# Per-head sums of an RWKV branch split into four 64x64 matmuls, and the second branch's first projection moved behind a fourth block of the first

## The reference

```
gates = jax.nn.sigmoid(p[..., i2:].reshape(B, S, N_BRANCH, D))
branch = jnp.einsum('bsnw,nwd->bsnd', ys, w_branch[l])
merged = jnp.sum(gates * branch, axis=2)
```

```
kk = kk / jnp.maximum(jnp.sqrt(jnp.sum(kk * kk, axis=-1, keepdims=True)), 1e-12)      # "length"
mu_y = jnp.mean(y, axis=-1, keepdims=True)                                            # "centre"
var_y = jnp.mean(jnp.square(y - mu_y), axis=-1, keepdims=True)                        # "var"
y = y + jnp.sum(r4 * k4 * r_k, axis=-1, keepdims=True) * v4                           # "bonus sum"
```

## Time and profile before

| | us |
|---|---|
| median of 3 runs | 2139.75 (2139.1 to 2139.93) |
| the profiled execution, its own time | 2138.36 |
| span of the profiled execution, first to last instruction | 2136.4 |
| mean granted TensorE clock | 0.998 of full |
| PE busy | 2105.1 (99%) |
| DVE busy | 1637.7 (77%) |
| ACT busy | 1232.5 (58%) |

### The profile page before, as it was taken

How to read it: one execution, slowest core, us unless ns; L and a number is a source line. 1 busy time by engine, 2 the same in 40 slices (tenths; PEclk the granted TensorE clock), 3 DMA queues, 4 the chain that set the end, 5 groups by cost and what they waited for, 6 DMA issues and landing times.

```text
span 2136.4 us, 39153 instructions
## 1 busy us (share of the span) xinstructions
PE 2105.1 (99%) x16336; PEld 1912.2 (90%) x16336; DVE 1637.7 (77%) x2517; ACT 1232.5 (58%) x2010; POOL 13.1 (1%) x20
## 2 busy tenths in 40 slices
PE   8999999999999999999999999999999999999999
PEld 6898999999998899998888889888898888998888
DVE  7899689887877688876887656887688764678875
ACT  4865556555855755555665447665476543666554
POOL 0000000000000000000000000000000000000000
PEclk9999999999999999999999999999999999999999
DMA  9565567777644477655555744555555566355553
GB/s 369 196 222 203 180 210 256 243 246 274 213 159 169 153 225 236 197 178 189 187 191 189 240 122 153 203 192 191 188 178 190 193 212 185 129 171 207 191 190 129
DMA packets 122098, 424.55 MB, mean 199 GB/s; under 512 B 13457, under 2 KB 22033, under 8 KB 121154
## 3 DMA queue, kind: packets, MB, share of 16 engines
q1 hardware_dynamic: 121922, 422.06, 58.9%
HBM read 417.68 MB, written 4.33 MB: 198 GB/s over the span
## 4 chain that ended last, share of the span: by engine, by line
PE 90%; ACT 4%; DVE 3%; DMA 2%; issue 1%; SPq 0%; POOL 0%; ACTq 0%; DVEq 0%
PE bank L207 89%; ACT arena L259 3%; DVE arena L214 1%; DMA raw<-W 1%; ACT hi L259 1%; DMA arena<-conv_rows 1%; PE bank L211 1%; DVE lo L214 1%; DVE ada L231 0%; ACT L259 0%; DVE arena L222 0%; SPq L204 0%; DMA xT<-x 0%; ACT L251 0%; POOL arena L214 0%
## 5 line engine op out<-in xcount | busy, mean ns | idle before, releaser
L207 PE MATMUL bank<-h,hi 128*128 128x256 f32 (+1 forms) x5216 | 1177.4, 312 | 0.0
L259 ACT ACTIVATE hi<-raw 128x1024 fp32r<-128x1024 f32 x656 | 689.2, 1057 | 575.9 <-PE bank L207 518.3
L207 PE MATMUL bank<-h,lo 128*128 128x256 f32 x3312 | 945.4, 285 | 0.3 <-DVE arena L222 0.3
L207 PEld LDWEIGHTS bank<-h,hi 128*128 128x128 f32 x5216 | 856.4, 190 | 61.0 <-issue 2.6
L214 DVE TENSOR_TENSOR lo<-raw,hi 128x1024 fp32r<-128x1024 f32 x656 | 792.0, 1220 | 122.1 <-ACT hi L259 121.3
L207 PEld LDWEIGHTS bank<-h,lo 128*128 128x128 f32 x3312 | 630.6, 190 | 12.0 <-issue 7.7
L207 PE MATMUL bank<-act,hi 128*128 128x512 f32 x1056 | 370.0, 393 | 0.0
L207 PE MATMUL bank<-act,lo 128*128 128x256 f32 x1056 | 294.7, 279 | 0.0
L207 PEld LDWEIGHTS bank<-act,hi 128*128 128x128 f32 x1056 | 197.9, 187 | 47.2
L207 PEld LDWEIGHTS bank<-act,lo 128*128 128x128 f32 x1056 | 197.9, 187 | 0.0
L259 ACT ACTIVATE arena<-arena 128x256 f32<-128x256 f32 (+4 forms) x202 | 98.6, 493 | 158.9 <-DVE arena L214 151.0
(11 more groups left out here) (155 smaller groups left out, 1977.2 us busy)
## 6 DMA issues: line engine op xcount, KB each, us to landing
raw<-W SPq DMA_DIRECT2D x664, 512.0 KB, 3.4
ada<-WA SPq DMA_DIRECT2D x80, 512.0 KB, 3.7
arena<-WA SPq DMA_DIRECT2D x16, 512.0 KB, 14.4
arena<-conv_rows SPq DMA_DIRECT2D x16, 280.0 KB, 6.7
arena<-taps SPq DMA_DIRECT2D x2, 1792.0 KB, 8.2
p_projected<-arena SPq DMA_DIRECT2D x2, 1024.0 KB, 8.0
arena<-scr SPq DMA_DIRECT2D x16, 128.0 KB, 4.8
arena<-p_projected SPq DMA_DIRECT2D x2, 1024.0 KB, 4.8
```

The costliest lines, as they stand in the source:

```text
L207: return self.done(lambda e: e.matmul(out, l, r, start=start, stop=stop, skip_group_check=True))
L259: return self.done(lambda e: e.activation(out, in_, f, scale=scale, **kw))
```

## The change

Each head sum becomes four matmuls of a 64x64 block by 512 columns (`head_sums`), all under one signal on the last. The first half of the columns goes to the same partitions as before, the second half crosses over: head s's second half lands on the partitions of the other head. Bank s holds what comes from head s. Both banks are taken ahead of the first matmul. The readers take four operations of 64 partitions by 512 columns in place of two of 128 by 512 (`sum_parts`), and a bank is free after its second-half operation. `var` on PE now waits for both halves of the squares. Apart from that, `branch0` 3 moves ahead of `finish(("rwkv", l))` and `branch1` 0, and `merge` 0 comes behind `branch0` 4.

```
-        s += [("branch0", l, 0), ("branch0", l, 1), ("branch0", l, 2), ("finish", ("rwkv", l)), ("pause if", (l, 4))]
-        s += [("branch1", l, 0), ("pause if", (l, 4)), ("branch0", l, 3), ("merge", l, 0), ("branch0", l, 4), ("branch1", l, 1), ("branch0", l, 5),
+        s += [("branch0", l, p) for p in range(4)] + [("finish", ("rwkv", l)), ("pause if", (l, 4))]
+        s += [("branch1", l, 0), ("pause if", (l, 4)), ("branch0", l, 4), ("merge", l, 0), ("branch1", l, 1), ("branch0", l, 5),
...
+        def sum_parts(name, l):
+
+            for half in range(2):
+                for s in range(2):
+                    use = (name, l, s)
+                    yield (half, use, slice(64 * s, 64 * s + 64), slice(half * 512, (half + 1) * 512),
+                           ps(use)[64 * (s ^ half):64 * (s ^ half) + 64, :])
...
+                def head_sums(uses, weight, x):
+
+                    outs = [take(GEN, use) for use in uses]
+                    for half in range(2):
+                        for s in range(2):
+                            rows, into = (slice(64 * t, 64 * t + 64) for t in (s, s ^ half))
+                            i = pe.mm(outs[s][into, :], C(weight)[rows, rows], x[rows, half * 512:(half + 1) * 512], True, True)
+                    i.then_inc(pe_rw, *uses)
...
-                        for half in range(2):
-                            o = take(GEN, ("length", l, half))
-                            pe.wait_ge(d_cst1, "cst1")
-                            pe.wait_ge(a_rw, ("square", l))
-                            pe.mm(o, C("bo"), Lc[:, half * 512:(half + 1) * 512], True, True).then_inc(
-                                pe_rw, ("length", l, half))
+                        pe.wait_ge(d_cst1, "cst1")
+                        pe.wait_ge(a_rw, ("square", l))
+                        head_sums([("length", l, s) for s in range(2)], "bo", Lc)
...
-                            pe.wait_ge(a_rw, ("centre sq", l, half))
-                            pe.mm(o, C("bom"), y2[:, half * 512:(half + 1) * 512], True, True).then_inc(
-                                pe_rw, ("var", l, half))
+                        pe.wait_ge(a_rw, ("centre sq", l, 1))
+                        head_sums([("var", l, s) for s in range(2)], "bom", y2)
...
-                        for half in range(2):
-                            sl = slice(half * 512, (half + 1) * 512)
-                            use = ("centre", l, half)
+                        for half, use, rows, cols, x in sum_parts("centre", l):
                             v.wait_ge(pe_rw, use)
-                            v.tt(yc[:, sl], Yt[:, sl], ps(use), SUB).then_inc(v_rw, use, frees=use)
+                            v.tt(yc[rows, cols], Yt[rows, cols], x, SUB).then_inc(
+                                v_rw, ("centre", l, half), frees=use if half else None)
```

More of the change, by code:

```diff
@@ L851, in step @@
                     elif what == "bonus sum":
-                        for half in range(2):
[L853 to L856, removed]
+                        pe.wait_ge(v_rw, ("bonus", l))
+                        head_sums([("bonus", l, s) for s in range(2)], "bo", a_)
                     elif what == "tok":
@@ L948, in step @@
                     elif what == "centre":
[L949 to L953, removed]
-                    elif what == "var":
-                        for half in range(2):
-                            o = take(GEN, ("var", l, half))
-                            pe.wait_ge(a_rw, ("centre sq", l, half))
-                            pe.mm(o, C("bom"), y2[:, half * 512:(half + 1) * 512], True, True).then_inc(
-                                pe_rw, ("var", l, half))
+                        pe.wait_ge(a_rw, ("y", l, 1))
+                        head_sums([("centre", l, s) for s in range(2)], "bom", Yt)
+                    elif what == "var":
+                        pe.wait_ge(a_rw, ("centre sq", l, 1))
+                        head_sums([("var", l, s) for s in range(2)], "bom", y2)
                 return step
@@ L1428, in step @@
                             v.wait_ge(d_pp, ("pp", 0))
[L1429 to L1432, removed]
+                        for half, use, rows, cols, x in sum_parts("length", l):
+                            v.wait_ge(pe_rw, use)
+                            v.ts(Ev[rows, cols], x, 1e-24, None, MAX).then_inc(
+                                v_rw, ("length", l, half), frees=use if half else None)
                         v.wait_ge(a_rw, ("exp w", l, 3))
@@ L1482, in step @@
                     elif what == "bonus sum":
[L1483 to L1485 removed]
+                        for half, use, rows, cols, x in sum_parts("bonus", l):
+                            v.wait_ge(pe_rw, use)
                             v.wait_ge(v_ln, ("ln", l, 1))
                             v.wait_ge(v_main, ("z", l, 11))
[L1488 to L1489 removed]
+                            v.tt(bon[rows, cols], x, vT[rows, cols], MUL).then_inc(
+                                v_rw, ("bon", l, half), frees=use if half else None)
                     elif what == "cross":
@@ L2224, in step @@
                     elif what == "var":
-                        for half in range(2):
-                            use = ("var", l, half)
+                        for half, use, rows, cols, x in sum_parts("var", l):
                             a.wait_ge(pe_rw, use)
-                            a.act(yv[:, half * 512:(half + 1) * 512], ps(use), ACT.Ln, bias=C("epsg")).then_inc(
-                                a_rw, ("ln var", l, half), frees=use)
+                            a.act(yv[rows, cols], x, ACT.Ln, bias=C("epsg")[rows, :]).then_inc(
+                                a_rw, ("ln var", l, half), frees=use if half else None)
                         for half in range(2):
```

2 lines of the change are left out of this document (removed).

## The result

The changed kernel takes 2142.36 us (median of 12 runs, 2140.12 to 2144.91) beside 2139.01 us (12 runs, 2134.72 to 2142.47) of the kernel before: a ratio of 1.0017 with a 95% interval of 1.0009 to 1.0025. It is slower by about 3.4 us, where I had predicted 0.6 us less. The time lies outside my range, and nearest to my second rival (DVE's lateness costs more: 2142). That it lies so near is in part luck: DVE's and ACT's lateness makes up about half of the difference, and the rest comes from a place that no rival named. The profiled execution after has 2143.27 us and a span of 2141.3.

A forecast was written before the change was run, and what follows sets the result against it. PE, busy 99% of the span, was taken to bound the kernel. Six terms, +0.1 +0.1 -0.6 -0.1 +0.7 -0.8, sum to -0.6 us from 2139.75: forecast 2139.1 us, range 2136.8 to 2141.6.

The forecast's parts named there:

- second rival: DVE and ACT lateness from the added readings reaches the end nearly in full: likely +2 us, +6 at worst; chance 0.13.
- Head sum on PE, 1.71 to 1.27: At each of eight head sums PE takes 1.27 us instead of 1.71, 0.44 less, including 0.41 for entering and leaving.
- The rival of quarters in turn: Quarters of 512 columns do not run together: 2.56 us a head sum against 1.71, +6.8 in all, 2146.5; chance 0.04.
- that of no price for entering and leaving: Head sums pay no 0.41 us around the quarters: 7.9 us less in all, 2131.9; chance 0.02.
- Two operations become four, each adding about 0.60 us to a run of them: Readers of head sums: +1.2 us of DVE for length, bonus sum, centre, and +1.2 of ACT for var, per layer.
- Layer 0, `length`, +0.1: Taking both banks first delays PE's start 0.73 us, which eats the 0.44 gained; some 0.2 of drain unpaid; net +0.1.
- Layer 0, `bonus sum`, +0.1: DVE's added 1.2 us meets 1.05 of slack; PE's 0.44 gain is spent waiting at the inverse's start; net +0.1.
- Layer 0, `centre`, `var`, `branch1` 0, -0.6: y1l comes 1.8 us late, its wait goes, but the splits of blocks 60 and 61 leave PE only 0.6 gained.
- Layer 1, `length`, -0.1: PE waits 0.49 us for the second bank against 0.44 gained, less what entering idle saves; net -0.1.
- Layer 1, `bonus sum`, +0.7: DVE's added 1.2 us meets 0.45 of slack, so PE's spatial stands 0.7 later; net +0.7 instead of -0.44.
- Layer 1, `centre` and `var`, -0.8: No PE wait for y1l or a split follows: 0.44 gained, and about 0.35 for var; net -0.8.
- bounds of the terms: First five terms between full gain and twice the cost, layer 1's end -0.9 to 0: -5.3 to about +3 us.

The follow-up runs named there:

- experiment 6: Kernel before, each head sum read in four operations of 64 partitions, both halves of head 0 before both of head 1; one run, 2142.86 us.
- x8: The kernel after, unchanged, run again for a second trace: 2142.56 us, ratio 1.0015.
- x11: The kernel after with 40 already fulfilled waits added to ACT's stream alone: 2141.84 us, ratio 1.0013.
- x15: The kernel after with bonus sum set back to before's form, plus 196 fulfilled waits in PE's stream and 40 in ACT's: 2139.86 us, ratio 1.0001.
- x9: The kernel before with the new order, and quarter sums only at layer 1's length, centre and var: 2139.83 us, ratio 1.0008.
- x12: The run of experiment 6: kernel before, head sums read in four 64-partition operations, head 0's halves first; 2142.86 us.
- x3: The kernel after with the old order, so only the head sums are changed: 2145.92 us, ratio 1.0028.
- x4: The kernel after with bonus sum set back on PE and DVE as it was before: 2141.84 us, ratio 1.0008.
- x7: The kernel after with 196 already fulfilled waits added to PE's stream: 2142.62 us, ratio 1.0018.

## Why the prediction was wrong

*Head sum on PE, 1.71 to 1.27.* Right, a little better: 1.21. The rival of quarters in turn is out (first four starts within 0.02 us, not over 0.1 apart), and so is that of no price for entering and leaving (0.50 gained, not 0.86).

*The step that failed: "Two operations become four, each adding about 0.60 us to a run of them", +1.2 us.* It measured +1.67 on DVE and +1.54 on ACT, since 0.60 is the spacing of operations that start on the same partition as the one before and these never do (experiment 6). The prediction had named this as a way to be wrong ("cost other than 0.6"), but its size was not in the range's terms. The trace of before had it. I looked at how long one 64-partition operation lasts (683 ns, as one of 128), which is not the spacing. DVE's timeline before, two operations on 64 partitions each (`unit`), first one half, then the other:

```profile
609.10 1.40 DVE L214 TENSOR_TENSOR arena<-arena,cst 64x512 f32<-64x512 f32 x2
```

1.40 for two is 0.71 from start to start and not 0.60.

*Layer 0, `length`, +0.1.* Not settled, and it can be far more. PE started on ACT's release as I said, 2.59 us idle where it was 0.96, but ACT was itself 0.5 late in this execution, and the start of the kernel scatters by up to 2.2 us over the traces. In three of the nine traces with a changed `length` in layer 0 (x8, x11, x15) PE went on at 1.2 GHz behind this idle time of 2.0 to 2.7 us; block 22 starts at 96.5 to 96.7 there, at 94.7 to 95.0 in the six others, at 94.5 to 95.6 in the ten without the change at this place, none of which shows the fall. That is a cost of the change that I had at nothing.

*Layer 0, `bonus sum`, +0.1.* +0.46. The 0.50 that PE gains is spent already at `cross`, where I had no wait of PE: its first 16 records ran together before, and now the second eight wait for DVE (PE is idle 0.22 ahead of 111.35). The inverse then costs another 0.49, with 0.63 of waiting for DVE.

*Layer 0, `centre`, `var`, `branch1` 0, -0.6.* The mechanism is right and the size decides the sign: +0.3 from block 29 to 61. I had put the chain 1.8 us late. Against PE (itself +0.54 at this point) ACT's Ln starts 1.17 late and not 0.6, and takes 1.54 more and not 1.2: 2.7. y1l's wait of 1.11 was saved, 0.4 came from `centre` and `var`, and blocks 60 and 61 took 1.81 back. With 0.9 more of lateness the -0.6 becomes +0.3.

*Layer 1, `length`, -0.1.* -0.5: no bank was late, so the 0.49 of wait did not come. PE came 0.93 us later than before in this pair, and ACT's eight readings that free the banks started at 549.74, as before (549.72). In x9, where PE was 0.3 early, they started at 548.12, and PE did not wait either; in x8 PE's weight load waited 0.26. So the term depends on where ACT's readings fall, and its size here is in part luck.

*Layer 1, `bonus sum`, +0.7.* +1.13, more by the 0.47 that I had too little for the readings.

*Layer 1, `centre` and `var`, -0.8.* About -0.4 by block starts: the wait for the second square is 0.56 and not 0.35, in both layers. In layer 0 it reads so, PE at `var` after:

```profile
249.21 1.09 PE L207 MATMUL bank<-arena,cst 64*64 64x512 f32 x8 [0.56 <-ACT arena L259]
```

Without `length` of layer 0 I had -0.7 for the mixers; they measure +0.9 in the pair of traces, +0.9 to +1.9 in the six traces of the kernel after and its padded forms. That is some 2 us of the 4 by which I missed. The other 2 us are behind them, at the two trips through DRAM, as longer waits and as lost clock. The prediction had nothing for them; it only said that it would be wrong "if a wait appears at a place not named here, in the FFN behind or in the loads". I gave that no chance of its own, and a range that was no wider for it. The bounds of the terms also add up to -4.4 and not to -5.3; the forecast does not hang on that.

## What to carry to other kernels

Price the readers of a split PSUM result by the spacing from start to start of operations that move from partition to partition, not by the length of one: here the emptying cost 1.67 us where the matmuls saved 0.50, and it is hidden only where the engine has that slack up to the next thing that PE needs. Follow each lateness to the second wait behind the one that is removed; there 0.9 us of lateness too little decided the sign. When a change of 0.1% is to be judged, compare block starts in two traces, and at each step tell the wait from the granted clock behind it: the waits of 2.7 to 5.8 us at the two trips were in 32 of 38 cases followed by a stretch at 1.2 GHz that cost another 1.3 to 2.9 us. Expect places that wait for DRAM to move by a microsecond or two when only the position of the instructions changes.

## What the runs showed of the hardware that was not expected

- ACT loses its overlap as DVE does when the start partition changes: four Ln of 64x512 take 2.81 us, 0.71 from start to start, where two of 128x512 took 1.27, 0.59 plus the last one's length. With the partition kept for two of them (x12) the same four have 0.59, 0.70, 0.59.
- Four f32 quarters of 512 columns run together: eight records in 1.11 us, plus 0.10 at the first main record behind.
- After a wait of 3.8 us (x3) for DVE's y1l PE ran at 1.2 GHz, 0.21 us for a main matmul and not 0.12, which added 1.5 us to the wait; after one of 1.34 (after) it ran at full clock. After 2.0 to 2.7 us of idle time at layer 0's `length` it did so in x8, x11 and x15 and not in after or x4. Behind the trips the same fall comes in some executions of a program and not in others (11.68 and 9.22 us in after and x8).
- PE's wait for a trip through DRAM is 1 to 2 us longer with other positions of the same instructions: 5.8, 4.9 and 5.4 us in the kernel after, x8 and x7, 3.9 and 3.3 with the padding in both streams. The Trainium skill (Advanced Engine Details and Errata, ISA Cache) gives 16 KB, or 256 instructions, for a line of the instruction cache; the 16 KB of PE's fetches agree, those of ACT are 8 KB here.
